# Softplus of the stick-breaking units in its symmetric form: the clip on VectorE goes, an absolute value on ScalarE comes

## The chip, the cores and the metric

One core of a Trainium2 chip runs the whole program. The metric is the device time of one execution in microseconds (us); less is better. The kernel before takes 1800.53 us, the median of three runs.

## What is computed

The program is a stack of transformer layers on 512 tokens of width 1024 in fp32. The change lies in the first layer, in its stick-breaking attention: 8 heads of width 64, blocks of 128 queries, each block against all keys up to its end.

```python
logits = einsum("bqhd,bkhd->bhqk", q_block, k[:, :k_end]) * scale
strict = (q_start + arange(128))[:, None] > arange(k_end)[None, :]
log_beta = log_sigmoid(logits)
log_keep = where(strict, log_sigmoid(-logits), 0.0)
log_tail = cumsum(log_keep, axis=3, reverse=True) - log_keep
weights = where(strict, exp(log_beta + log_tail), 0.0)
out = einsum("bhqk,bkhd->bqhd", weights, v[:, :k_end])
```

Since log_sigmoid(-x) = -softplus(x), a softplus of every logit is wanted. All else in the program (another attention before it, projections, three feed-forward blocks, two more layers' attention) is the same in both kernels.

## The kernel before

The whole program is written out by hand: each of the engines TensorE (PE), VectorE (DVE), ScalarE (ACT), GpSimd (POOL) and SyncE (SP) has one list of instructions in a fixed order, and semaphores join the lists. An engine that waits at one instruction does nothing that stands behind it.

The stick-breaking attention is worked off in 16 units, `SB_UNITS`. Unit u is a pair of heads p = u // 4 and a step r = u % 4 over the keys, the last block of keys first. Its logits are [128 keys, 2 heads, 128 (r + 1) queries], so the units of a pair hold 256, 512, 768 and 1024 elements a partition. They lie in PSUM at `sb_psum(u)`, in two banks of their own for each r. What the engines do for unit u:

- PE, `sb_qk(u)` (L1048, and L1051 for the mask, which adds a large negative number where a key isn't strictly before its query): the logits x. It waits until the weights of unit u - 4 have been read (`sb_weights`).
- DVE, L2521: `sb_clip(u)` = min(x, 40) into one of two buffers in `tmp` (`sb_clamped`).
- ACT, `softplus` (L1607, L1609): Exp and then Ln(1 + .) in place on that buffer (`sb_exped`, `sb_logged`).
- DVE, `sb_larger(u)` (L2484): max(x, that) into `sb_pl`, one of three buffers (`sb_plus`). This is softplus(x), since above 40 softplus(x) is x.
- PE, `sb_tail_sum(u)` (L1061 with a triangle, and L1070 with ones for the units of the pair so far): the suffix sums, added onto the logits in PSUM. Where r is 2 or more the ones meet a running sum that DVE makes in `sb_add` (L2499, L2500).
- ACT, `sb_weigh(u)` (L1772): Exp of that, from PSUM into `sb_w`.
- PE, `sb_values(p)` (L1079), once for each pair, one unit late: the weights against the values, into bank 6. ACT, `sb_save(p)` (L1778), copies it out, and PE's `sb_qk` of a unit with r = 3 waits for that copy.

The order on the engines: for u = 0 to 17 ACT does sb_weigh(u - 2), softplus(u), and sb_save at u = 5, 9 and 13 (then, at u = 8, 12 and 16, a square of the saved tile). DVE does sb_larger(u - 1), clip(u), sb_add(u - 1), but where u % 4 is 3 the clip(u) comes ahead of sb_larger(u - 1). PE does sb_tail_sum(u) and, after it, sb_qk(u + 3), except that sb_qk of r = 3 stands in the middle of the tail sum two units before. Other work lies among these: at u = 0 ACT squares a tile and splits a weight chunk (L1502), at u = 1 it takes a square root, for which it loads another table of functions and then the first again (L1796); at u = 12 ACT and DVE scale and split four tiles; and at u = 15 PE does part of the product with w_out (L868 to L870). Behind the last unit the root over the attention's output is needed before PE can go on.

Of the kernel before, what the change touches and what calls it, by code (L numbers as in the profile page):

```python
# [15 lines left out]
ALU = mybir.AluOpType  # L16
AXIS = mybir.AxisListType
ACT = mybir.ActivationFunctionType

P = 128  # L20
SEQ = 512
# [15 lines left out]
CLAMP = 40.0  # L37
# [30 lines left out]
ADD0 = {name: sum(n - 1 for _, n in NORMS[:i]) for i, (name, _) in enumerate(NORMS)}  # L68
# [33 lines left out]
def program(nc, a, out):  # L102
    ctx = ExitStack()
    with ctx:
        def at(name, shape, offset, dt=FP32):
            return nc.alloc_sbuf_tensor_at(name, shape, dt, offset=offset)

        def sem(name):
            return ctx.enter_context(nc.semaphore(name))
# [13 lines left out]
        sb_pl = at("sb_pl", [P, 3, 2, SEQ], o_act)  # L123
# [193 lines left out]
        def modv(section, t):  # L317
# [39 lines left out]
        sq_added = sem("sq_added")  # L357
# [12 lines left out]
        mem_diag, mem_tile, mem_done, mem_saved = (  # L370
            sem("mem_diag"), sem("mem_tile"), sem("mem_done"), sem("mem_saved"))
# [22 lines left out]
        out_hi, q_tile, q_saved = sem("out_hi"), sem("q_tile"), sem("q_saved")  # L394
        mem_q_saved = sem("mem_q_saved")

        sb_scores, sb_clamped, sb_exped, sb_logged, sb_plus = (
            sem("sb_scores"), sem("sb_clamped"), sem("sb_exped"), sem("sb_logged"), sem("sb_plus"))
        sb_tail, sb_weights, sb_out, sb_saved, sb_added = (
            sem("sb_tail"), sem("sb_weights"), sem("sb_out"), sem("sb_saved"), sem("sb_added"))  # L400

# [331 lines left out]
        SB_UNITS = 4 * 4  # L733

        def sb_unit(u):

            p, r = u // 4, u % 4
            return p, r, P * (3 - r)

        def sb_psum(u):  # L740

            b = (2, 4, 0, 6)[u % 4]
            return banks[:, b:b + 2, sb_unit(u)[2]:SEQ]

        SB_OUT = 6

        def sb_clip(u):

            return tmp[:, 2 * (u % 2):2 * (u % 2) + 2, sb_unit(u)[2]:SEQ]

# [744 lines left out]
        def _(act):  # L1495
# [8 lines left out]
            def split_at(c, n=2048):  # L1504
                split_w(c, c % 2, 16 * (c // 2 + 1), n)
# [11 lines left out]
            def square(name, t, src, ready):  # L1517
                n = NORM[name]
                act.wait_ge(*ready)
                if t == 0:  # L1520
                    if n:
                        act.wait_ge(sum_ready, n)
                    act.activation(sq_sum[:, :], src, ACT.Square).then_inc(sq_ready, 1)
                else:
                    if t >= 3:
                        act.wait_ge(sq_added, ADD0[name] + t - 2)
                    act.activation(squares_of(name, t), src, ACT.Square).then_inc(sq_ready, 1)

            def root(name):
                n, count = NORM[name], NORMS[NORM[name]][1]  # L1530
                act.wait_ge(sum_ready, n + 1)
                act.activation(rms[:, :], norm_bank(name), ACT.Sqrt, scale=-1.0 / (P * count), bias=eps)\
                    .then_inc(root_ready, 1)

            def high(name, t, dst, bias=None, buf=tmp):

                act.wait_ge(scaled, SPLIT0[name] + t + 1)
                act.activation(dst, buf[:, t % 4, :], ACT.Identity,
                               bias=bias if bias is not None else 0.0).then_inc(act_hi_done, 1)
# [61 lines left out]
                    if beside:  # L1601
                        beside(t)

            def softplus(t, clamped, exped, logged, n):

                act.wait_ge(clamped, n)
                act.activation(t, t, ACT.Exp).then_inc(exped, 1)  # L1607
                act.wait_ge(exped, n)
                act.activation(t, t, ACT.Ln, bias=1.0).then_inc(logged, 1)  # L1609

# [155 lines left out]
            def sb_weigh(u):  # L1766

                p, r, q0 = sb_unit(u)
                act.wait_ge(sb_tail, u + 1)
                if p >= 2 and r == 0:  # L1770
                    act.wait_ge(sb_out, p - 1)
                act.activation(sb_w[:, p % 2, :, P * r * (r + 1) // 2:P * (r + 1) * (r + 2) // 2],  # L1772
                               sb_psum(u), ACT.Exp).then_inc(sb_weights, 1)

            def sb_save(p):

                act.wait_ge(sb_out, p + 1)
                act.activation(o_raw[1][:, p, :], bank[SB_OUT], ACT.Copy).then_inc(sb_saved, 1)  # L1778

            def square_b(p):  # L1780
                square("ob", p, o_raw[1][:, p, :], (sb_saved, p + 1))

            for u in range(SB_UNITS + 2):
                if u >= 2:
                    sb_weigh(u - 2)
                if u < SB_UNITS:
                    softplus(sb_clip(u), sb_clamped, sb_exped, sb_logged, u + 1)
                if u == 0:
                    square("oa", 3, o_raw[0][:, 3, :], (out_saved, 4))
                    split_at(C0["w_out"] + 1)  # L1790
                if u in (5, 9, 13):
                    sb_save(u // 4 - 1)
                if u == 1:
                    act.preload_act_table(ACT.Sqrt)
                    root("oa")
                    act.preload_act_table_set("natural_log_exp_and_others")  # L1796
                if u in (8, 12, 16):
                    square_b(u // 4 - 2)
                if u == 12:
                    for t in range(4):  # L1800
                        high("w_out", t, o_hi_0[0][:, t, :], buf=rel[0])
# [140 lines left out]
        def _(dve):  # L1942
# [306 lines left out]
            for t in range(NT):  # L2249
                if t:  # L2250
                    dve.wait_ge(x_squared, t)
                dve.tensor_tensor_reduce(out=x_junk, in0=x_tok[:, t, :], in1=x_tok[:, t, :], scale=1.0,
                                         scalar=0.0, op0=ALU.mult, op1=ALU.add,
# [33 lines left out]
            def mem_save(c, m):  # L2287
                dst = (kmT_0, vm_0)[c % 2][c // 2]
                dve.wait_ge(mem_done if m else mem_tile, c + 1)
                return dve.tensor_copy(dst[:, m, :], bank[mem_bank(c, m)][:, 0:NMEM])  # L2290
# [12 lines left out]
            for n in range(4):  # L2303
# [6 lines left out]
                                     op0=ALU.add, op1=ALU.add).then_inc(scaled, 8)  # L2310
# [165 lines left out]
            def sb_larger(u):  # L2476

                p, r, q0 = sb_unit(u)
                dve.wait_ge(sb_logged, u + 1)
                if u == 0:  # L2480
                    dve.wait_ge(chunk_done, C0["w_out"])
                if u >= 3:
                    dve.wait_ge(sb_tail, u - 1 if r == 3 else u - 2)
                dve.tensor_tensor(sb_pl[:, u % 3, :, q0:SEQ], sb_psum(u), sb_clip(u), ALU.max)\  # L2484
                    .then_inc(sb_plus, 1)

            def sb_add(u):

# [21 lines left out]
                                  ALU.subtract).then_inc(act_ready, 1)  # L2510

            for u in range(SB_UNITS + 1):
                if u and u % 4 != 3:
                    sb_larger(u - 1)
                if u < SB_UNITS:
                    if u == 0:
                        dve.wait_ge(sq_added, ADD0["oa"] + 2)
                    if u == 2:
                        mem_save(1, 1).then_inc(mem_saved, 1)
                    dve.wait_ge(sb_scores, u + 1)  # L2520
                    dve.tensor_scalar(sb_clip(u), sb_psum(u), CLAMP, None, ALU.min).then_inc(sb_clamped, 1)  # L2521
                if u % 4 == 3:
                    sb_larger(u - 1)
                if u and (u - 1) % 4 in (1, 2):
                    sb_add(u - 1)
                if u == 1:
                    mem_save(1, 0).then_inc(mem_saved, 1)
                    add_squares("oa", 3)
                    split_w(C0["w_out"] + 1, 1)
                if u in (13, 16):  # L2530
                    add_squares("ob", 1 + u // 16)
                for n in {4: (0,), 5: (1,), 8: (2,), 9: (3,)}.get(u, ()):
                    c = P * n
                    dve.wait_ge(root_ready, NORM["oa"] + 1)
                    part = dve.reciprocal(rms[:, c:c + P], rms[:, c:c + P])
                    if n == 3:
                        part.then_inc(rms_ready, 1)
                if u == 12:
                    dve.wait_ge(rms_ready, NORM["oa"] + 1)
                    for t in range(4):  # L2540
                        scale_a(t)
                    low_a(0)
                    low_a(1)
                if u == 13:
                    low_a(2)
                    low_a(3)
# [38 lines left out]
            for t in range(KT):  # L2585
                dve.scalar_tensor_tensor(out=x[:, t, :], in0=x[:, t, :], scalar=gain("final_g", t),
                                         in1=rms[:, :], op0=ALU.mult, op1=ALU.mult).then_inc(x_ready, 1)
            split_w(C0["a_q"], 0)
            for t in range(NT):
                dve.wait_ge(av_saved, NT + t + 1)  # L2590
                if t:
                    dve.wait_ge(v_ss, t)
                dve.tensor_tensor_reduce(out=vsq_junk[:, :], in0=vtok_a[:, t, :], in1=vtok_a[:, t, :], scale=1.0,
                                         scalar=0.0, op0=ALU.mult, op1=ALU.add,
# [39 lines left out]
            for ct in range(6):  # L2634
# [4 lines left out]
                for lo, hi, g in gm_parts(ct):  # L2639
                    dve.scalar_tensor_tensor(  # L2640
                        out=tmp[lo:hi, ct % 2, :].rearrange("p (n t) -> p n t", t=P),
                        in0=gm_bank(ct)[lo:hi, :].rearrange("p (n t) -> p n t", t=P),
                        scalar=vec[lo:hi, VEC0["a_v_norm_2"] + ct:VEC0["a_v_norm_2"] + ct + 1],
                        in1=bs[lo:hi, g, :].rearrange("p (o t) -> p o t", o=1)
# [161 lines left out]
```

## Time and profile before

| | |
|---|---|
| median of 3 runs | 1800.53 us |
| the three runs | 1802.06, 1800.53, 1800.51 us |
| the profiled execution: its time | 1800.57 us |
| its span, first to last instruction | 1798.9 us |
| TensorE's granted clock, mean over the span | 0.999 of full speed |
| span of the stick-breaking stage | about 214 us to 287 us from the start |

The span is what the trace covers; 1.67 us lie around it. Times in the trace are microseconds from the start of the span. PEld is TensorE's loading of weights, which overlaps its products. "Idle before" is the time in which an engine stood still just ahead of an instruction, and the name behind it is what ended that.

### The profile page before, as it was taken

The numbers are of one execution on the slowest core, as the hardware profiler recorded it, in microseconds if no ns is written. First come the engines' busy times: TensorE is split into PE (matmuls) and PEld (weight loads), VectorE is DVE, ScalarE is ACT, GpSimd is POOL, SyncE is SP. The second block draws the span as 40 slices with busy tenths as digits, with TensorE's granted clock in tenths as the row PEclk, the third lists the DMA queues.
The fourth block names the chain that finished last, engine by engine and source line by source line (L and its number), as shares of the span: only waits on it lengthen the run. The fifth ranks groups of instructions, "written<-read, shape, count | busy, mean of one in ns | idle before, by whom it ended". The sixth has DMA issues, their size and how long they took to land.

```text
span 1798.9 us, 22457 instructions
## 1 busy us (share of the span) xinstructions
PE 1768.7 (98%) x8312; PEld 1428.7 (79%) x8312; DVE 1096.3 (61%) x1598; ACT 733.2 (41%) x1030; POOL 40.6 (2%) x78
## 2 busy tenths in 40 slices
PE   7999999999999999999999999999999999999998
PEld 6887547888888888878888888889766888888887
DVE  6878775655556335775677674245577567677423
ACT  7313663333444223444344443233365434444322
POOL 4110000000000000000000000000000000000000
PEclk9999999999999999999999999999999999999999
DMA  9794203232222323312322222323401232222231
GB/s 345 266 340 139 80 21 111 75 106 94 93 93 87 111 82 98 112 48 94 117 93 93 93 93 84 109 83 106 170 24 48 74 114 93 93 93 93 94 105 70
DMA packets 149081, 195.29 MB, mean 109 GB/s; under 512 B 3646, under 2 KB 133000, under 8 KB 146332
## 3 DMA queue, kind: packets, MB, share of 16 engines
q1 hardware_dynamic: 140696, 154.23, 26.4%
q0 software_dynamic: 7600, 39.13, 5.9%
q10 hardware_dynamic: 724, 1.10, 0.2%
q8 instruction: 41, 0.67, 0.2%
q14 instruction: 20, 0.16, 0.0%
HBM read 189.15 MB, written 5.29 MB: 108 GB/s over the span
## 4 chain that ended last, share of the span: by engine, by line
PE 92%; DVE 4%; DMA 2%; ACT 1%; issue 1%; POOL 0%; DVEq 0%; ACTq 0%
PE bank L805 20%; PE bank L807 20%; PE bank L806 20%; PE bank L868 3%; PE bank L870 3%; PE bank L869 3%; PE bank L1475 2%; PE bank L1474 2%; PE bank L1476 2%; PE bank L952 2%; PE bank L1004 1%; PE bank L848 1%; PE bank L973 1%; PE bank L849 1%; PE bank L850 1%; PE bank L1061 1%
## 5 line engine op out<-in xcount | busy, mean ns | idle before, releaser
L1947 DVE TENSOR_TENSOR w_lo<-w_stage,w_hi 128x2048 fp32r<-128x2048 f32 (+3 forms) x136 | 299.0, 2198 | 436.3 <-ACT w_hi L1502 436.0
L805 PE MATMUL bank<-act_hi,w_hi 128*128 128x512 f32 x1216 | 475.2, 391 | 1.5 <-DVE act_lo L2322 0.6
L807 PE MATMUL bank<-act_hi,w_lo 128*128 128x512 f32 x1216 | 473.3, 389 | 0.0
L806 PE MATMUL bank<-act_lo,w_hi 128*128 128x512 f32 x1216 | 473.1, 389 | 0.0
L1502 ACT ACTIVATE w_hi<-w_stage 128x2048 fp32r<-128x2048 f32 (+3 forms) x138 | 253.6, 1837 | 466.0 <-PE bank L807 335.6
L805 PEld LDWEIGHTS bank<-act_hi,w_hi 128*128 128x128 f32 x1216 | 228.2, 188 | 50.7 <-DVE act_lo L2011 2.1
L806 PEld LDWEIGHTS bank<-act_lo,w_hi 128*128 128x128 f32 x1216 | 228.3, 188 | 47.7 <-issue 0.5
L807 PEld LDWEIGHTS bank<-act_hi,w_lo 128*128 128x128 f32 x1216 | 228.2, 188 | 47.7
L805 PE MATMUL bank<-mid_hi,w_hi 128*128 128x512 f32 x352 | 136.9, 389 | 0.0
L806 PE MATMUL bank<-mid_lo,w_hi 128*128 128x512 f32 x352 | 136.9, 389 | 0.0
L807 PE MATMUL bank<-mid_hi,w_lo 128*128 128x512 f32 x352 | 136.9, 389 | 0.0
L1649 ACT ACTIVATE mid_hi<-tmp 128x512 f32 x66 | 40.7, 633 | 97.1 <-DVE tmp L2157 97.1
L806 PEld LDWEIGHTS bank<-mid_lo,w_hi 128*128 128x128 f32 x352 | 66.1, 188 | 13.8
L805 PEld LDWEIGHTS bank<-mid_hi,w_hi 128*128 128x128 f32 x352 | 66.1, 188 | 13.8
L807 PEld LDWEIGHTS bank<-mid_hi,w_lo 128*128 128x128 f32 x352 | 66.1, 188 | 13.6
L1474 PE MATMUL bank<-w_hi,mid_hi 128*128 128x512 f32 x176 | 68.8, 391 | 0.0
L1476 PE MATMUL bank<-w_lo,mid_hi 128*128 128x512 f32 x176 | 68.5, 389 | 0.0
L1475 PE MATMUL bank<-w_hi,mid_lo 128*128 128x512 f32 x176 | 68.5, 389 | 0.0
L1639 ACT ACTIVATE tmp<-tmp,vec 128x512 f32<-128x512 f32 x44 | 33.5, 809 | 70.0 <-DVE tmp L1969 70.0
L1639 ACT ACTIVATE mid_val<-tmp,vec 128x512 f32 x44 | 33.5, 808 | 69.8 <-DVE tmp L1969 69.8
L1969 DVE SCALAR_TENSOR_TENSOR tmp<-bank,rms 128x512 f32<-128x512 f32 x88 | 56.4, 682 | 0.0
L2161 DVE TENSOR_TENSOR mid_lo<-tmp,mid_hi 128x512 f32 x66 | 42.7, 689 | 9.4 <-ACT mid_hi L1649 9.4
(412 smaller groups left out, 2622.8 us busy)
## 6 DMA issues: line engine op xcount, KB each, us to landing
ada_stage<-in_w_ada POOLq DMA_DIRECT2D x24, 1024.0 KB, 7.4
w_stage<-in_w_up SPq DMA_DIRECT2D x22, 1024.0 KB, 5.0
w_stage<-in_a_ffn_in SPq DMA_DIRECT2D x22, 1024.0 KB, 5.0
w_stage<-in_b_ffn_in SPq DMA_DIRECT2D x22, 1024.0 KB, 5.1
w_stage<-in_w_in SPq DMA_DIRECT2D x10, 1024.0 KB, 7.6
w_stage<-in_b_ffn_out SPq DMA_DIRECT2D x10, 1024.0 KB, 5.1
w_stage<-in_w_down SPq DMA_DIRECT2D x8, 1024.0 KB, 5.1
w_stage<-in_a_ffn_out SPq DMA_DIRECT2D x8, 1024.0 KB, 5.1
```

Of the source, the lines that this page charges most:

```text
L805: pe.matmul(dst, wh, mh, start=start and k == 0, stop=False)
L806: pe.matmul(dst, wh, ml, start=False, stop=False)
L807: last = pe.matmul(dst, wl, mh, start=False, stop=stop and k == nk - 1)
L868: pe.matmul(dst, wh, mh, start=start and k == ks[0], stop=False)
L869: pe.matmul(dst, wh, ml, start=False, stop=False)
L1474: pe.matmul(dst, mh, hi[:, k, :], start=j == 0 and k == 0, stop=False)
L1475: pe.matmul(dst, ml, hi[:, k, :], start=False, stop=False)
L1476: last = pe.matmul(dst, mh, lo[:, k, :], start=False, stop=j == 5 and k == nk - 1)
L1502: act.activation(w_hi[slot][:, 0:n], raw[:, 0:n], ACT.Copy).then_inc(w_hi_done, 1)
L1639: act.activation(conv_tile(f, i, s, m), conv_src(f, s, m)[:, :], ACT.Identity, scale=w2, bias=b).then_inc(tap_started, 1)
L1947: dve.tensor_tensor(w_lo[slot][:, 0:n], raw[:, 0:n], w_hi[slot][:, 0:n].bitcast(FP32), ALU.subtract).then_inc(w_ready, 1)
L1969: return dve.scalar_tensor_tensor(out=dst, in0=src[:, :], scalar=scale, in1=norm[:, :], op0=ALU.mult, op1=ALU.mult)
```

## The change

The softplus is taken as max(x, 0) + log(1 + exp(-|x|)). ScalarE takes |x| from PSUM (`sb_size`), then Exp with a scale of -1, then Ln as before; VectorE's clip goes, and its `sb_larger` becomes one instruction that takes the maximum with 0 and adds. Since VectorE no longer has a step for unit u, `sb_larger(u - 1)` isn't behind one either for any u. The copies of the output (`sb_save`) stay where they are, on ScalarE.

```diff
-        def sb_clip(u):
+        def sb_abs(u):
...
-            def softplus(t, clamped, exped, logged, n):
+            def softplus(t, clamped, exped, logged, n, sign=1.0):
                 act.wait_ge(clamped, n)
-                act.activation(t, t, ACT.Exp).then_inc(exped, 1)
+                act.activation(t, t, ACT.Exp, scale=sign).then_inc(exped, 1)
...
+            def sb_size(u):
+
+                act.wait_ge(sb_scores, u + 1)
+                if u == 0:
+                    act.wait_ge(sq_added, ADD0["oa"] + 2)
+                if u >= 2:
+                    act.wait_ge(sb_plus, u - 1)
+                act.activation(sb_abs(u), sb_psum(u), ACT.Abs).then_inc(sb_sized, 1)
...
                 if u >= 2:
                     sb_weigh(u - 2)
                 if u < SB_UNITS:
-                    softplus(sb_clip(u), sb_clamped, sb_exped, sb_logged, u + 1)
+                    sb_size(u)
+                    softplus(sb_abs(u), sb_sized, sb_exped, sb_logged, u + 1, -1.0)
...
-                dve.tensor_tensor(sb_pl[:, u % 3, :, q0:SEQ], sb_psum(u), sb_clip(u), ALU.max)\
-                    .then_inc(sb_plus, 1)
+                dve.scalar_tensor_tensor(out=sb_pl[:, u % 3, :, q0:SEQ], in0=sb_psum(u), scalar=0.0,
+                                         in1=sb_abs(u), op0=ALU.max, op1=ALU.add).then_inc(sb_plus, 1)
...
             for u in range(SB_UNITS + 1):
-                if u and u % 4 != 3:
+                if u:
                     sb_larger(u - 1)
-                if u < SB_UNITS:
-                    if u == 0:
-                        dve.wait_ge(sq_added, ADD0["oa"] + 2)
-                    if u == 2:
-                        mem_save(1, 1).then_inc(mem_saved, 1)
-                    dve.wait_ge(sb_scores, u + 1)
-                    dve.tensor_scalar(sb_clip(u), sb_psum(u), CLAMP, None, ALU.min).then_inc(sb_clamped, 1)
-                if u % 4 == 3:
-                    sb_larger(u - 1)
+                if u == 2:
+                    mem_save(1, 1).then_inc(mem_saved, 1)
                 if u and (u - 1) % 4 in (1, 2):
                     sb_add(u - 1)
```

## Rows read from the trace of the kernel before

**Rows 1.** The page: busy time by engine, the last chain by engine, one group of instructions

```profile
PE 1768.7 (98%) x8312; PEld 1428.7 (79%) x8312; DVE 1096.3 (61%) x1598; ACT 733.2 (41%) x1030; POOL 40.6 (2%) x78
...
PE 92%; DVE 4%; DMA 2%; ACT 1%; issue 1%; POOL 0%; DVEq 0%; ACTq 0%
...
L1969 DVE SCALAR_TENSOR_TENSOR tmp<-bank,rms 128x512 f32<-128x512 f32 x88 | 56.4, 682 | 0.0
```

**Rows 2.** Busy time of each engine in two stretches, with granted clock

```profile
217.00:230.00 13.00, 12.67 (x62) 8.74 (x61) 9.90 (x15) 12.00 (x15) 0.55 (x1) 1.00 0.30 102
...
243.00:256.00 13.00, 13.00 (x66) 6.81 (x65) 7.68 (x13) 7.84 (x13) 0.00 (x0) 1.00 0.01 1
```

**Rows 3.** Timeline of ScalarE, first units: start, us, instruction, idle before

```profile
215.48 1.28 ACT L1764 ACT_TABLE_LOAD   x1
...
221.16 1.28 ACT L1794 ACT_TABLE_LOAD   x1
...
224.45 0.38 ACT L1772 ACTIVATE sb_w<-bank 128x256 f32<-128x256 f32 x1
...
226.13 0.84 ACT L1609 ACTIVATE tmp<-tmp 128x768 f32<-128x768 f32 x1
```

**Rows 4.** Pieces of the chain that ended last, in order of time: start, us, what

```profile
228.02 1.56 PE bank L1061 x4
...
234.38 0.84 PE bank L1048 x4
...
242.77 1.56 PE bank L1061 x4
...
246.04 1.77 PE bank L1061 x4
247.82 1.29 PE bank L1070 x4
249.11 0.85 PE bank L1048 x4
...
250.67 2.30 PE bank L1079 x16
...
257.50 1.56 PE bank L1061 x4
...
272.22 1.56 PE bank L1061 x4
...
276.02 1.72 PE bank L1061 x4
```

**Rows 5.** Timeline of VectorE, units 6 and 7

```profile
240.63 1.23 DVE L2521 TENSOR_SCALAR tmp<-bank 128x1024 f32<-128x1024 f32 x1 [1.88 <-PE bank L1051]
241.77 0.95 DVE L2484 TENSOR_TENSOR sb_pl<-bank,tmp 128x768 f32<-128x768 f32 x1
...
244.06 1.23 DVE L2484 TENSOR_TENSOR sb_pl<-bank,tmp 128x1024 f32<-128x1024 f32 x1 [0.42 <-ACT tmp L1609]
```

**Rows 6.** Timeline of ScalarE, units 5 to 7

```profile
238.30 0.60 ACT L1778 ACTIVATE ob_raw<-bank 128x512 f32<-128x512 f32 x1 [1.68 <-PE bank L1079]
...
239.93 0.84 ACT L1609 ACTIVATE tmp<-tmp 128x768 f32<-128x768 f32 x1
241.13 0.60 ACT L1772 ACTIVATE sb_w<-bank 128x512 f32<-128x512 f32 x1 [0.35 <-PE bank L1070]
...
242.97 1.06 ACT L1609 ACTIVATE tmp<-tmp 128x1024 f32<-128x1024 f32 x1
```

**Rows 7.** Groups by line and shape, 200 to 300 us: busy us, mean ns, idle before

```profile
L1772 ACT ACTIVATE sb_w<-bank 128x1024 f32<-128x1024 f32 x4 | 4.1, 1018 | 7.0 <-PE bank L1070 7.0
...
L1772 ACT ACTIVATE sb_w<-bank 128x768 f32<-128x768 f32 x4 | 3.2, 812 | 4.3 <-PE bank L1070 4.3
...
L2504 DVE SCALAR_TENSOR_TENSOR rel<-oa_raw,vec,rms 128x512 f32<-128x512 f32 x4 | 2.7, 746 | 0.0
```

**Rows 8.** The instructions of line 2521, the clip: ns min/median/max

```profile
L2521 DVE TENSOR_SCALAR tmp<-bank x16: 414/814/1225, 213.9 to 270.1; 128x256 f32<-128x256 f32 x4, 128x512 f32<-128x512 f32 x4, 128x768 f32<-128x768 f32 x4, 128x1024 f32<-128x1024 f32 x4
```

More of the change, by code:

```diff
@@ L395, in program @@
         mem_q_saved = sem("mem_q_saved")
-        sb_scores, sb_clamped, sb_exped, sb_logged, sb_plus = (
-            sem("sb_scores"), sem("sb_clamped"), sem("sb_exped"), sem("sb_logged"), sem("sb_plus"))
+        sb_scores, sb_sized, sb_exped, sb_logged, sb_plus = (
+            sem("sb_scores"), sem("sb_sized"), sem("sb_exped"), sem("sb_logged"), sem("sb_plus"))
         sb_tail, sb_weights, sb_out, sb_saved, sb_added = (
```

## The prediction

> **What bounds the kernel now.** I read the page first. TensorE is busy for 1768.7 of 1798.9 us, and 92% of the chain that ended last is its work [rows 1]: the kernel is one long line of products, and a change elsewhere counts only where TensorE comes to stand and wait. Next, the busy times in windows of the stick-breaking stage. In the first units (217 to 230 us) ScalarE is busy for 12.00 of 13 us, in a later pair of heads (243 to 256) for 7.84 [rows 2]; VectorE has room in both. So ScalarE's room for one more step is not the same everywhere. Last, the chain and the two timelines. Three times TensorE stands still ahead of the tail sum of a unit with r = 2, at 242.77, 257.50 and 272.22, with 14.73 and 14.72 us between them [rows 4]: that distance is the period of a pair. What it waits for is sb_larger(6), which starts at 241.77 though its Ln ended at 239.93 + 0.84 = 240.77; the clip of unit 7 lay ahead of it from 240.63 [rows 5, 6]. Elsewhere in the pair TensorE doesn't wait.
>
> **What goes.** 16 clips on VectorE, four of each size, median 814 ns [rows 8]: 13.0 us of VectorE's time. Of this only the clips of units 3, 7, 11 and 15 lie on the path, and with them gone sb_larger(6) could start 1.0 us sooner. That is the gain: at most 1 us a pair.
>
> **What comes.** 16 times Abs on ScalarE, from PSUM into SBUF. No row shows an Abs. The nearest rows are sb_weigh, which is an activation of the same shapes over the same route: 0.38 us for 256 elements [rows 3], 0.60 for 512 [rows 6], 0.81 and 1.02 for 768 and 1024 [rows 7]; and sb_save, a Copy, is 0.60 for 512 as well [rows 6]. I take these, since Exp and Copy cost the same: 4 × 2.81 = 11.2 us more on ScalarE. Each Abs stands between sb_weigh(u - 2) and Exp(u). Where two neighbours in a queue don't depend on each other, the next starts about 0.1 before the end of the one before (on VectorE 241.77 against 240.63 + 1.23 [rows 5]); Abs now starts so behind sb_weigh, as Exp did, and Exp starts 0.03 after the end of Abs, as Ln after Exp. So every unit's way is longer by its Abs and 0.03. Bounds: an Abs that took no time, below; above, the pass from SBUF (Ln, 1.06 for 1024 [rows 6]), 0.04 more each.
>
> Exp with a scale of -1 and Ln keep their durations. sb_larger becomes a SCALAR_TENSOR_TENSOR. With an immediate scalar and a source in PSUM it takes 682 ns for 512 elements [rows 1], which is what the clip and the maximum of such a row cost (0.95 for 768, 1.23 for 1024 [rows 5]): nothing more. With a scalar from a tile it takes 746 [rows 7], the upper bound, 0.06 more.
>
> The new waits of Abs(u), for sb_scores and for sb_larger(u - 2), end early: the logits of unit 7 are there before the old clip starts at 240.63 [rows 5], and Abs(7) comes some 3 us later. That of sq_added at u = 0 ends before the table load at 215.48 is over. Behind the Abs stand Exp, Ln and the next sb_weigh; VectorE's sb_larger and then TensorE's tail sum wait for them.
>
> **The sum, first units.** Here ScalarE is the bound. Abs(0) adds 0.38 + 0.03 and Abs(1) 0.60 + 0.03, so sb_weigh(0) goes from 224.45 [rows 3] to 225.49 and ends at 225.87. Abs(2) 225.77 to 226.58, Exp(2) to 227.45, Ln(2) to 228.32 (it was 226.13 + 0.84 = 226.97 [rows 3]), sb_larger(2) 228.35 to 229.30. The tail sum of unit 2 starts at 229.34 instead of 228.02 [rows 4]: **+1.32**. Then sb_weigh(1) to 228.82, Abs(3) to 229.74, Exp(3) 230.83, Ln(3) 231.92, sb_larger(3) 233.18. TensorE, done with unit 2 and sb_qk(5) at 232.61, has to wait for this. A tail sum of 768 elements takes 1.56 after a wait [rows 4], where three quarters of the 1.72 that 1024 take would be 1.29; so a wait costs 0.27 of filling, and after one 1024 take some 1.99. Tail sum 3 is done at 233.22 + 1.99 + 1.29 = 236.50; it was 234.38, where sb_qk(6) starts [rows 4]: **+2.12**. Covers are gone from here on.
>
> **The sum, a pair.** Everything up to the values of pair 0 is late by 2.12, so sb_save(0) starts at 238.30 + 2.12 = 240.42 [rows 6] and ends at 241.02. sb_weigh(4) to 241.30, Abs(6) to 242.01, Exp 242.88, Ln 243.75, sb_larger(6) 244.73, tail sum 6 at 244.77, for 242.77 before: +2.00. The clip that no longer lies ahead of sb_larger(6) pays for the Abs, and 0.12 is over. But then: sb_weigh(5) to 244.25, Abs(7) to 245.17, Exp 246.26, Ln(7) 247.35 (it was 242.97 + 1.06 = 244.03 [rows 6]), sb_larger(7) 248.61. Tail sum 7 starts at 248.65, not 246.04 [rows 4], and TensorE is free 0.6 before that: the wait moves from r = 2 alone to r = 2 and r = 3. Its end is 251.93 for 249.11: **+2.82**, 0.70 more than a pair ago. The period can be read in one loop, from Ln(6) to Ln(10): sb_weigh(5) 0.50, Abs(7) 0.92, Exp and Ln(7) 2.18, sb_larger(7) 1.26, tail sum 7 0.04 + 1.99 + 1.29, sb_qk(10) 1.07, tail sum 8 0.50, values 2.30, sb_save 0.65, sb_weigh(8) 0.28, Abs(10) 0.71, Exp and Ln(10) 1.74, together 15.4 against 14.7. So pair 2 ends at +3.5.
>
> **The sum, last pair.** At u = 12 the four scaled tiles hold ScalarE as before, and TensorE still finds its inputs there. Tail sum 14 comes at values(2) + 4.4 = 275.6 for 272.22 (+3.4; without sb_qk behind it TensorE had waited longer here before), and tail sum 15, where part of the product with w_out gives cover, at about 279.5 for 276.02: **+3.5 to +3.7**. Behind it values, sb_save, the root and the scaling follow one another with no slack, and after that TensorE is the bound, so nothing is given back. I take +3.6.
>
> The profiled execution of before took 1800.57 (1798.9 + 1.67), 0.04 over the median of its runs. 1800.53 + 3.6 gives 1804.1 us. About 10 Abs lie on this path, so each 0.1 us by which one differs from my rows moves the result by 1.0 to 1.2. With both upper bounds (0.04 and 0.06 for each) it is +4.4. With an Abs of no time it is -1.7.
>
> The Trainium skill speaks against the change: the page "ScalarE: Activation LUTs", section "Rules for kernel authors", wants such cheap operations on VectorE, which it calls up to three times faster in bf16. The rows here are fp32 from PSUM and don't show that (clip 1.23 us for 1024 elements, ScalarE 1.02); what makes the change dear by my sum is the place in ScalarE's queue, not the rate.
>
> **The rivals.** (a) *The wait goes and nothing takes its place.* If Abs(7), Exp and Ln of unit 7 were hidden behind TensorE's work, the wait of some 1 us at three units would go. For it speaks that ScalarE stands idle for 5 of 13 us in a pair [rows 2]; against it that this idle time lies behind, not ahead of, the chain from sb_weigh(5) to Ln(7). It decides at an Abs 0.4 us shorter than my rows (no change in total), and at the bound of no time it gives 1798.9.
> (b) *Part of the delay is taken back*: Abs runs somewhat shorter, or the waits overlap. At 0.1 to 0.2 us less for each, 1801.9 to 1802.8.
> (c) *Abs brings table loads.* A load is 1.28 us [rows 3]; two a unit, to it and back, are 32 × 1.28 = 41 us, nearly all on the path: 1845. Against it: Copy runs between Exps with no load around it [rows 6].
> The same page, section "Table sets: the hidden batching unit", lists abs as a filler in every set, so that no load would come. No row of before shows an Abs.
> (d) *More than the sum*: dearer gaps between dependent activations, 0.1 instead of 0.03 on each Abs, and both upper bounds above: 1805 to 1806. That the longer waits make the granted clock fall is not likely, for it is 1.00 in both windows [rows 2].
>
> **Numbers.** My forecast, +3.0 to +4.4, has 0.72; (a) 0.04, (b) 0.13, (c) 0.02, (d) 0.09. The range of 8 in 10 takes in (b) in part and most of (d): 1801.8 to 1806.0. A measurement of this kernel can tell about 0.2%, 3.6 us, from no change, and my sum lies just there: I give half of the forecast's 0.72 to each side. Slower by over 0.2%: 0.37 + 0.11 = 0.48. Within: 0.35 + 0.13 + 0.02 = 0.50. Faster: 0.02.
>
> **What would show it.** In the profile after: 16 Abs with 0.38, 0.60, 0.81, 1.02 us and no new table load; sb_weigh(0) near 225.5; tail sum 3 ending near 236.5; the distance of the tail sums of units 6, 10 and 14 near 15.4; TensorE waiting for sb_larger at r = 2 and r = 3. I am wrong if Abs has another duration, if the wait at r = 3 is absent, or if the delay at 287 us is not that of the end.

## The result and the profile after

The changed kernel takes 1805.47 us in the median of 12 runs (1804.21 to 1808.47), the kernel before 1801.00 over 12 runs (1800.51 to 1802.06): a ratio of 1.0024, 95% interval 1.0015 to 1.0032. That is 4.5 us more, or 0.24%. It is just over the 0.2% named in the prediction, but the interval reaches to both sides of that mark. 1804.1 was forecast, within 1801.8 to 1806.0. The measured time lies in that range, but above the forecast's own band of +3.0 to +4.4, where the prediction had its rival (d).

The first lines of the page after: busy time by engine, and the shares of the chain that ended last.

```profile
PE 1771.0 (98%) x8312; PEld 1430.0 (79%) x8312; DVE 1084.7 (60%) x1582; ACT 743.2 (41%) x1046; POOL 40.6 (2%) x78
...
PE 91%; DVE 4%; ACT 2%; issue 1%; DMA 1%; SPq 0%; DVEq 0%; ACTq 0%
```

Against [rows 1]: VectorE does 16 instructions and 11.6 us less, ScalarE 16 and 10.0 us more, and ScalarE has 2% of the chain where it had 1%. TensorE's work is the same 8312 products, yet its busy time is 2.3 us more. The prediction's sum has only the filling after a wait for this; 1.5 us of it are one tail sum at a lower clock, which comes up below.

The groups by shape, 200 to 300 us, have the durations of Abs (busy us, mean ns, idle before), of which the kernel before has none:

```profile
L1787 ACT ACTIVATE tmp<-bank 128x1024 f32<-128x1024 f32 x4 | 4.1, 1015 | 0.0
...
L1787 ACT ACTIVATE tmp<-bank 128x768 f32<-128x768 f32 x4 | 3.3, 815 | 0.0
...
L1787 ACT ACTIVATE tmp<-bank 128x512 f32<-128x512 f32 x4 | 2.4, 588 | 0.0
```

They are those of sb_weigh for the same shapes [rows 7], 1018 and 812 ns. The timeline of ScalarE in the first units (start, us, instruction), to be held against [rows 3]:

```profile
215.42 1.28 ACT L1764 ACT_TABLE_LOAD   x1
216.72 0.38 ACT L1787 ACTIVATE tmp<-bank 128x256 f32<-128x256 f32 x1
217.13 0.42 ACT L1607 ACTIVATE tmp<-tmp 128x256 f32<-128x256 f32 x1
...
225.44 0.38 ACT L1772 ACTIVATE sb_w<-bank 128x256 f32<-128x256 f32 x1
225.72 0.81 ACT L1787 ACTIVATE tmp<-bank 128x768 f32<-128x768 f32 x1
226.55 0.84 ACT L1607 ACTIVATE tmp<-tmp 128x768 f32<-128x768 f32 x1
227.43 0.84 ACT L1609 ACTIVATE tmp<-tmp 128x768 f32<-128x768 f32 x1
```

Exp starts 0.02 to 0.03 us after the end of Abs, no table load stands between them, and sb_weigh(0) is at 225.44 where it was at 224.45 (225.49 was forecast). What TensorE makes of this is in its timeline; in brackets is the idle time before. These are all its waits for sb_larger:

```profile
229.32 2.23 PE L1061 MATMUL bank<-sb_pl,neg_upper 128*128 128x384 f32 x4 [1.60 <-DVE sb_pl L2494]
...
245.57 1.56 PE L1061 MATMUL bank<-sb_pl,neg_upper 128*128 128x384 f32 x4 [0.94 <-DVE sb_pl L2494]
...
249.42 1.98 PE L1061 MATMUL bank<-sb_pl,neg_upper 128*128 128x512 f32 x4 [0.57 <-DVE sb_pl L2494]
...
260.98 1.56 PE L1061 MATMUL bank<-sb_pl,neg_upper 128*128 128x384 f32 x4 [0.94 <-DVE sb_pl L2494]
...
264.82 1.98 PE L1061 MATMUL bank<-sb_pl,neg_upper 128*128 128x512 f32 x4 [0.57 <-DVE sb_pl L2494]
...
276.44 1.56 PE L1061 MATMUL bank<-sb_pl,neg_upper 128*128 128x384 f32 x4 [1.58 <-DVE sb_pl L2494]
```

Two things are to be read here. The waits at r = 2 (768 elements, "128x384" a head) have stayed, and those at r = 3 ("128x512") have come to them; the distance of the waits at r = 2 is 15.41 and 15.46 us against 14.73 and 14.72 [rows 4]. And the first row, tail sum 2, takes 2.23 us where the same four products take 1.56 everywhere else. The windows say why (start and end, length, busy us of PE, PEld, DVE, ACT, POOL, then the granted clock, 1.00 being full speed):

```profile
217.00:229.30 12.30, 10.64 (x55) 7.30 (x53) 6.26 (x10) 12.05 (x17) 0.55 (x1) 1.00 0.32 108
229.30:233.30 4.00, 3.98 (x10) 2.27 (x10) 2.31 (x4) 2.49 (x4) 0.00 (x0) 0.59 0.00 1
233.30:238.30 5.00, 5.00 (x21) 2.36 (x22) 1.95 (x3) 2.88 (x6) 0.00 (x0) 0.98 0.00 0
```

Behind the 1.60 us of waiting TensorE had the lower of its two clock levels, 1.2 GHz, for most of 4 us. Narrower windows show when:

```profile
227.70:229.30 1.60, 0.01 (x1) 0.00 (x0) 0.96 (x2) 1.60 (x3) 0.00 (x0) 1.00 0.06 18
229.30:230.00 0.70, 0.68 (x2) 0.49 (x3) 0.70 (x2) 0.67 (x2) 0.00 (x0) 1.00 0.02 6
230.25:233.25 3.00, 3.00 (x9) 1.55 (x7) 1.37 (x2) 1.56 (x2) 0.00 (x0) 0.50 0.00 0
233.50:238.30 4.80, 4.80 (x21) 2.16 (x20) 1.75 (x3) 2.68 (x6) 0.00 (x0) 1.00 0.00 0
```

The clock is full during the wait and for the first 0.7 us of products behind it, and falls only then, with TensorE busy. In the kernel before the clock is 1.00 in this stage. So the profiled execution, 1805.20 us, holds one such fall; how often the runs do is a question for the experiments.

### The profile page after: what moved, and what is told of

The parts are those of the page before. It is cut to its first block, busy times and chain, and to the rows that moved or that the text cites. A ratio compares the mean times of both kernels' runs of the same rounds, so it can differ in the third digit from the quotient of the medians.

```text
span 1803.5 us, 22471 instructions
## 1 busy us (share of the span) xinstructions
PE 1771.0 (98%) x8312; PEld 1430.0 (79%) x8312; DVE 1084.7 (60%) x1582; ACT 743.2 (41%) x1046; POOL 40.6 (2%) x78
## 4 chain that ended last, share of the span: by engine, by line
PE 91%; DVE 4%; ACT 2%; issue 1%; DMA 1%; SPq 0%; DVEq 0%; ACTq 0%
PE bank L805 20%; PE bank L807 20%; PE bank L806 20%; PE bank L868 3%; PE bank L870 3%; PE bank L869 3%; PE bank L1476 2%; PE bank L1475 2%; PE bank L1474 2%; PE bank L952 2%; PE bank L1004 1%; PE bank L973 1%; PE bank L848 1%; PE bank L849 1%; PE bank L850 1%
```

## The experiments

A measure of its own was wanted, since half a microsecond is less than the scatter of times. In each trace I take the stretch from the start of ScalarE's copy ahead of the first units (L1567, oa_raw) to the start of its root behind the last (L1532, rms). Everything that the change touches lies in it, and what happens in the 214 us ahead doesn't. That matters: from trace to trace the stretch starts anywhere between 214.49 and 216.57 us, while what lies behind it is 1512.2 to 1512.6 us in all of them. The stretch is 286.57 - 214.86 = 71.71 us before and 291.08 - 214.81 = 76.27 after: +4.56. In the table "reckoned" is what was forecast for the kernel, "stretch" the difference of the stretch to 71.71, one trace each, and "median" the difference to the median of the kernel before in the same session (11 runs of each kernel, 5 of the one with every Abs twice).

```
kernel                               reckoned  stretch   median   ratio, 95% interval
the change                             +3.6     +4.56     +4.5    1.0024 (1.0015-1.0032)
Abs on VectorE in the clip's place      0       -0.03     +0.7    1.0000 (0.9991-1.0009)
clip kept, sb_larger always first      +3.2     +3.06     +3.0    1.0017 (1.0008-1.0026)
change in pair 0 alone                 +2.1     +2.09     +3.6    1.0019 (1.0010-1.0028)
change in pairs 1 to 3 alone           +1.5     +1.61     +1.5    1.0008 (0.9999-1.0017)
Abs ahead of sb_weigh                  +2.3     +2.53     +2.1    1.0013 (1.0004-1.0022)
copies on VectorE                      +2.2     +2.60     +2.0    1.0014 (1.0004-1.0023)
both                                   +0.1     +0.39     -0.3    1.0001 (0.9992-1.0010)
change, TensorE's first wait filled  +3.6-4.0   +3.72     +3.4    1.0019 (1.0010-1.0029)
every Abs twice                       +10.8    +12.66    +12.1    1.0078 (1.0064-1.0091)
pick: clip for pair 0 and r = 2        -1.5     -1.34     -1.8    0.9992 (0.9983-1.0001)
pick: clip for pair 0, copies moved    -1.5     -1.47     -2.1    0.9991 (0.9982-1.0000)
pair 0 alone, first wait filled      +2.0-2.3   +2.08     +1.6    1.0012 (1.0003-1.0021)
```

The cuts of code below are against the kernel before in the first two experiments and against the changed kernel in the others; "..." stands for lines left out.

**Formula or place.** The symmetric formula with its absolute value on VectorE, in the place and order of the clip. |x| is taken there by clearing the sign bit.

```diff
-                    dve.tensor_scalar(sb_clip(u), sb_psum(u), CLAMP, None, ALU.min).then_inc(sb_clamped, 1)
+                    dve.tensor_scalar(sb_abs(u).bitcast(mybir.dt.int32), sb_psum(u).bitcast(mybir.dt.int32),
+                                      0x7fffffff, None, ALU.bitwise_and).then_inc(sb_clamped, 1)
```

> The symmetric softplus with its absolute value on VectorE, in the place and order of the old clip; Exp with scale -1 and the new sb_larger stay. If the loss comes from where Abs stands in ScalarE's queue, this costs nothing: within 0.3 us of the kernel before, tail sums of units 2, 6, 10 and 14 at the times of before (228.0, 242.8, 257.5, 272.2), and no fall of the clock. If the formula itself costs (Exp with a scale, an add more in sb_larger), some 1 us or more stays. If the order of sb_larger had been the cause, this is 0 as well.

The stretch is 71.68 us, that of before to 0.03. The timeline of TensorE has the waits of before, in their places [rows 4]:

```profile
228.04 1.56 PE L1070 MATMUL bank<-sb_pl,neg_upper 128*128 128x384 f32 x4 [0.26 <-DVE sb_pl L2502]
...
242.79 1.56 PE L1070 MATMUL bank<-sb_pl,neg_upper 128*128 128x384 f32 x4 [1.04 <-DVE sb_pl L2502]
```

The median is 0.7 higher, with an interval of 0.9991 to 1.0009; nothing in the trace answers to it. Exp with a scale of -1 and the combined sb_larger cost nothing: the whole loss is that of the move to ScalarE, or of the order.

**The order.** The old formula and clip, and only sb_larger(u - 1) always ahead of the clip of u.

```diff
-                if u and u % 4 != 3:
+                if u:
                     sb_larger(u - 1)
...
-                if u % 4 == 3:
-                    sb_larger(u - 1)
```

> The old formula with the old clip, only sb_larger(u - 1) is always ahead of clip(u), as in the changed kernel. The text of the change makes this look like the part that helps. By the same reckoning from durations as the prediction's: sb_larger(6) is 1 us sooner, but clip(7) now lies behind it, so Exp(7), Ln(7) and sb_larger(7) come later and TensorE waits at r = 3: +0.6 after tail sum 6, +2.1 after tail sum 7, +3.2 us in all. The rival, that the clip ahead of sb_larger was what held TensorE, gives -1 us for each of three units, -3 us.

+3.06, not -3. In this trace the stretch starts 0.83 us later than in that of before, and so do all times in it. VectorE's timeline (first fence) and ScalarE's (second) around unit 7 show the exchange:

```profile
243.11 0.96 DVE L2506 TENSOR_TENSOR sb_pl<-bank,tmp 128x768 f32<-128x768 f32 x1 [2.06 <-ACT tmp L1618]
243.99 1.22 DVE L2548 TENSOR_SCALAR tmp<-bank 128x1024 f32<-128x1024 f32 x1
```

```profile
245.24 1.06 ACT L1616 ACTIVATE tmp<-tmp 128x1024 f32<-128x1024 f32 x1 [1.21 <-DVE tmp L2548]
```

sb_larger(6) now comes at once, but clip(7) behind it lets Exp(7) wait for 1.21 us, where it had been 0.16 before. In pairs 1 and 2 TensorE now waits for 1.30 us at r = 3 instead of 1.04 at r = 2; pair 0 has a new wait of 1.29 at r = 3, and the last pair 0.70 and 0.76 in place of 1.68. So the clip in front of sb_larger was the right order as long as there was a clip. The change can put sb_larger first only because it leaves no clip behind it.

**The first units and the others.** The new form for units 0 to 3 alone, and for 4 to 15 alone; the others keep clip, maximum and order.

```diff
+        def sb_new(u):
+            return u < 4          # the other kernel: u >= 4
...
+                    if sb_new(u):
+                        sb_size(u)
...
+                if not sb_new(u):
+                    dve.tensor_tensor(sb_pl[:, u % 3, :, q0:SEQ], sb_psum(u), sb_abs(u), ALU.max)\
+                        .then_inc(sb_plus, 1)
+                    return
```

> The change for units 0 to 3 alone; units 4 to 15 have the clip as before. My sum: +2.1 us, all of it by the end of tail sum 3, and nothing after it. If the granted clock falls after the wait ahead of tail sum 2, as in the profile of the changed kernel, +2.9. If the loss were spread evenly over the units (a cost for each Abs), a quarter of it by time of work: +1.1.

> The change for units 4 to 15 alone. My sum: +1.5 us (0.7 a pair for two pairs, little in the last), the clock at full speed throughout, distance of tail sums 6, 10 and 14 of 15.4 against 14.7 us. By an even cost of each Abs: +3.4. Together with the run for pair 0 it should add to the whole change.

The stretches are +2.09 and +1.61, together +3.70. So four of 16 units have more than half of the loss, as ScalarE's 12.00 of 13 us in [rows 2] had let one expect. In the profile of pair 0 alone the clock stays up, and the sum of the prediction can be read in TensorE's timeline without it:

```profile
229.29 1.56 PE L1070 MATMUL bank<-sb_pl,neg_upper 128*128 128x384 f32 x4 [1.60 <-DVE sb_pl L2509]
...
233.14 1.98 PE L1070 MATMUL bank<-sb_pl,neg_upper 128*128 128x512 f32 x4 [0.57 <-DVE sb_pl L2509]
```

Forecast were 229.34 and 233.22, and 1.99 for the second. But the median, +3.6, is 1.5 above this trace, and six of its eleven runs are over 1.5 us above the fastest: that calls for a second cause, which the profiled execution didn't meet. The mean granted clock of each run hints at the clock: it is 0.998 in five of those six and 0.999 in the five others.

**The queue.** From unit 2 on Abs(u) ahead of sb_weigh(u - 2); the copies of pairs 0 to 2 on VectorE; both together.

```diff
+                if 2 <= u < SB_UNITS:
+                    sb_size(u)
                 if u >= 2:
                     sb_weigh(u - 2)
```

```diff
-                if u in (5, 9, 13):
-                    sb_save(u // 4 - 1)
...
+                if u in (6, 10, 14):
+                    dve.wait_ge(sb_out, u // 4)
+                    dve.tensor_copy(o_raw[1][:, u // 4 - 1, :], bank[SB_OUT]).then_inc(sb_saved, 1)
```

> The changed kernel, but from unit 2 on Abs(u) stands ahead of sb_weigh(u - 2) instead of behind it. If the place in ScalarE's queue is the cause, an Abs that falls into ScalarE's wait for a tail sum is hidden: for r = 0 and 1 there is such a wait, for r = 2 and 3 there is hardly one, since there ScalarE is what sets the pace. Reckoned as in the prediction: +0.4 by tail sum 3 less than the change, distance of tail sums 6, 10 and 14 of 15.15 instead of 15.4 us, +2.3 us to before in all where the change has +3.5. If the mere work of ScalarE is the bound, moving it changes nothing (+3.5).

> The changed kernel, but the copies of the output (sb_save of pairs 0 to 2) are on VectorE. ScalarE then no longer stands waiting for the values (2.3 us on TensorE) and for its copy ahead of sb_weigh(4), so the loop of 15.4 us is cut between tail sum 8 and Abs(10): the wait at r = 2 goes, that at r = 3 grows to 1.3 us, distance 15.0 us, +2.2 us in all. By the rival that VectorE's copy is itself late for sb_qk of r = 3: no better than the change.

> Both: Abs ahead of sb_weigh, and the copies on VectorE. Reckoned: 1.4 to 1.5 us lost in the first units (these are not touched by it), then a distance of 14.4 us, less than the 14.7 of before, and +0.1 us in all: equal to the kernel before. If the two gains were the same time counted twice, +2.

The same 16 Abs with the same durations cost +2.5, +2.6 and +0.4. With both moves the waits at r = 2 beyond pair 0 are gone, and the distance of tail sums 7, 11 and 15 is 14.38 and 14.43 us, under the 14.7 of before:

```profile
248.26 1.98 PE L1061 MATMUL bank<-sb_pl,neg_upper 128*128 128x512 f32 x4 [0.69 <-DVE sb_pl L2495]
...
262.64 1.98 PE L1061 MATMUL bank<-sb_pl,neg_upper 128*128 128x512 f32 x4 [0.69 <-DVE sb_pl L2495]
...
277.07 1.98 PE L1061 MATMUL bank<-sb_pl,neg_upper 128*128 128x512 f32 x4 [0.87 <-DVE sb_pl L2495]
```

ScalarE's timeline in the same kernel has Abs(7) straight behind a wait, ahead of sb_weigh(5), and Exp(7) right behind sb_weigh(5):

```profile
243.41 1.02 ACT L1787 ACTIVATE tmp<-bank 128x1024 f32<-128x1024 f32 x1 [1.42 <-PE bank L1051]
244.33 0.59 ACT L1772 ACTIVATE sb_w<-bank 128x512 f32<-128x512 f32 x1
244.80 1.06 ACT L1607 ACTIVATE tmp<-tmp 128x1024 f32<-128x1024 f32 x1
```

The forecasts for the three kernels were 0.2 to 0.4 us too low. The order of ScalarE's work, and not its amount, is what the change costs in pairs 1 to 3.

**How much each Abs counts.** Every Abs is done a second time, on its own result.

```diff
-                act.activation(sb_abs(u), sb_psum(u), ACT.Abs).then_inc(sb_sized, 1)
+                act.activation(sb_abs(u), sb_psum(u), ACT.Abs).then_inc(sb_half, 1)
+                act.wait_ge(sb_half, u + 1)
+                act.activation(sb_abs(u), sb_abs(u), ACT.Abs).then_inc(sb_sized, 1)
```

> The changed kernel with every Abs done twice, the second time in place in SBUF (the absolute value of an absolute value, so nothing of the result changes). 11.2 us more on ScalarE. With my account all but the last of it lies on the path: each unit's way is longer by its Abs again, TensorE waits at r = 1, 2 and 3, +7 us more than the change, about +10.8 us to before. If ScalarE's idle time took it up, +1 to +3 more than the change. If all of it and more counted, +11 more.

The stretch grows by 8.1 us over the change's for some 12 us more on ScalarE, where 7 had been reckoned: some two thirds of this further work lie on the path. The second pass reads SBUF and starts 0.03 after the first, which I had left out of the reckoning. A fall of the clock, as after, is in this trace too (the first four products of tail sum 2 take 2.06 us, after a wait of 2.57).

**The clock.** Two products more on TensorE in the first wait, into columns that nobody reads; first in the changed kernel ahead of tail sum 2, then in that of pair 0 alone, ahead of the logits of unit 4.

```diff
+                if u == 2:
+                    for n in range(2):
+                        pe.matmul(bank[2][:, 0:384], neg_upper[:, :], qkv[:, 16, 0:384], start=False,
+                                  stop=True, skip_group_check=True)
                 sb_tail_sum(u)
```

> The changed kernel with two products more on TensorE in the wait ahead of tail sum 2 (into columns of a bank that nobody reads; 1.3 us of work in a wait of 1.6), which change no time by themselves. If a fall of the granted clock after that wait is what lifts the median of the changed kernel 0.9 us over my sum, the runs lie closer together and the median is 0.5 to 0.9 us under the change's 1805.5; the profile has the clock at full speed. If the fall has no part in it, the time is the change's, or up to 0.3 above.

> The kernel with the change in pair 0 alone, and two products more on TensorE (1.3 us) ahead of the logits of unit 4, so that TensorE waits some 0.3 us ahead of tail sum 2 and not 1.6. Nothing that the chain needs comes later by them. Without them it was 1804.5 us in the median, but 1802.7 in the profiled execution, where the clock stayed up. If a fall of the clock is what lies between the two, the median comes down to 1802.8 to 1803.5, +2.0 to +2.3 to before. If the scatter has another cause, it stays near 1804.5.

With the fill the wait ahead of tail sum 2 is 0.26 us, and the clock is 1.00 in the whole stage:

```profile
230.15 1.56 PE L1061 MATMUL bank<-sb_pl,neg_upper 128*128 128x384 f32 x4 [0.26 <-DVE sb_pl L2498]
```

The stretch is +3.72, which is 0.84 less than the change's, and the prediction's sum was +3.6. The fill costs nothing itself: pair 0 alone has +2.08 with it and +2.09 without. Set against this execution of the change, the fall cost 0.84 us. But two traces without the fill, that of pair 0 alone and that with the copies on VectorE, wait for the same 1.60 us at the same place and keep their clock. The window that was at 0.59 in the change reads in the first of them:

```profile
229.30:233.30 4.00, 3.43 (x15) 2.01 (x16) 2.31 (x4) 3.20 (x4) 0.00 (x0) 1.00 0.00 0
```

1.00, and 15 products in the time of 10. So the fall came in one of three traces with this wait: the wait doesn't force it. The medians agree in direction: 1805.47 goes to 1804.82 with the fill (ratios 1.0024 and 1.0019), and pair 0 alone from +3.6 to +1.6 (1.0019 and 1.0012). But the intervals overlap, and the kernel before was 1800.93 in the one session and 1801.66 in the other. As a whole the profiled execution with the fill, 1805.45 us, wasn't faster than the change's, 1805.20, for its stretch starts at 215.65 us and not at 214.81. That the fall costs 0.84 us in the trace that has it is shown. That it makes the scatter of the runs, and that the fill takes it away, isn't shown. The runs without a profile don't say where the clock fell, and there is a second place: in the first 50 us it is 0.97 in three traces, those with clip and sb_larger first, with both moves and with the fill, and 1.00 in the others. Pair 0 alone with the fill still has two runs of eleven at 1805.2 and 1805.5 with mean clocks of 0.997 and 0.998.

**What they point to.** The clip stays where ScalarE has no room. First: pair 0 and r = 2 keep the clip, the rest has Abs ahead of sb_weigh. Second: pair 0 alone keeps it, Abs ahead of sb_weigh, copies on VectorE.

```diff
         def sb_new(u):
+            return u >= 4 and u % 4 != 2          # the second: u >= 4
```

> What the experiments point to: the clip on VectorE stays for pair 0, where ScalarE is the bound, and for r = 2; the new form with Abs ahead of sb_weigh for r = 0, 1 and 3 of pairs 1 to 3. Copies stay on ScalarE. sb_larger(6) isn't behind a clip any more, and Abs(7) lies in time that ScalarE has. Reckoned: -1.5 us to before. The rival: the wait only moves to r = 3, 0.

> The clip stays for pair 0 alone; pairs 1 to 3 have the new form with Abs ahead of sb_weigh, and the copies are on VectorE. It is the run with both moves, less what that lost in the first units: -1.5 us to before. If that loss doesn't go with pair 0, 0.

The stretches are -1.34 and -1.47 us, the medians 1799.38 and 1799.12 against 1801.20: a tenth of a per cent, and both intervals just reach 1. TensorE's waits in the first of the two, ahead of tail sums 2, 7, 11 and 14:

```profile
228.23 1.56 PE L1070 MATMUL bank<-sb_pl,neg_upper 128*128 128x384 f32 x4 [0.25 <-DVE sb_pl L2508]
...
245.73 1.98 PE L1070 MATMUL bank<-sb_pl,neg_upper 128*128 128x512 f32 x4 [0.43 <-DVE sb_pl L2511]
...
260.14 1.98 PE L1070 MATMUL bank<-sb_pl,neg_upper 128*128 128x512 f32 x4 [0.43 <-DVE sb_pl L2511]
...
270.91 1.56 PE L1070 MATMUL bank<-sb_pl,neg_upper 128*128 128x384 f32 x4 [0.73 <-DVE sb_pl L2508]
```

1.8 us of waiting are left of the 4.0 of before (0.26, 1.04, 1.04 and 1.68 in the trace with Abs on VectorE, whose stretch is that of before). Of these 2.2 us 1.34 reach the stretch; where the rest goes wasn't followed.

## Why the prediction was right, point by point

- *Abs costs what sb_weigh costs.* 815 and 1015 ns for 768 and 1024 elements; right, and so were the 0.03 to Exp. The Trainium skill, page "ScalarE: Activation LUTs", section "Table sets: the hidden batching unit", names abs as a filler of every set; the trace agrees, with no load between the Abs and Exp rows above and 21 table loads in the program before and after. Rival (c) is out.
- *The new sb_larger and Exp cost nothing.* Shown by Abs on VectorE: -0.03 us. That kernel is also the answer to the Trainium skill, page "ScalarE: Activation LUTs", section "Rules for kernel authors", which wants relu, max, min, add and mul on VectorE. The clip, a min, is one of these; an absolute value isn't in the list. VectorE is the better place in this kernel, but not by speed: there the step takes 1226 ns for 1024 elements (the row below, Abs on VectorE), on ScalarE 1015.

```profile
L2541 DVE TENSOR_SCALAR tmp<-bank 128x1024 int32<-128x1024 int32 x4 | 4.9, 1226 | 5.0 <-PE bank L1060 4.9
```

- *First units, +1.32 and +2.12.* With the clock up, tail sum 2 starts at 229.29 and tail sum 3 at 233.14 (pair 0 alone), each within 0.1 of the forecast, and the stretch is +2.09.
- *A pair, 15.4 us.* 15.41 and 15.46; the waits are 0.94 at r = 2 and 0.57 at r = 3, and the latter was forecast at 0.6. Pairs 1 to 3 alone give +1.61, for a sum of +1.5.
- *Nothing is given back after the stage.* The stretch is +4.56 and the span of the trace 4.6 us longer (1803.5 against 1798.9).
- *The last pair.* Tail sum 14 starts at 276.44. Less the 0.84 of the fall that is 275.60, and 275.6 was forecast.
- *+3.6 in all.* +3.72 in the trace with the fill, in which the clock stays up. Of the change's +4.56, 0.84 is the fall.
- *The clock.* This is the step that failed. I wrote under (d) that a fall of the granted clock "is not likely", on the evidence of two windows at 1.00. It was thin evidence: TensorE stands still for 0.33 us in the one and not at all in the other, and the waits of 1.04 and 1.68 us of that trace lie outside both. The clock fell in the profile, after 1.60. Of the 1.4 us between 1804.1 and 1805.47, 0.5 is that twelve runs of before lie at 1801.0 and not at the 1800.53 of three; the other 0.9 has the size of the fall in that one trace, which doesn't show that it is the fall in the twelve. Its price was small, since while TensorE ran slowly its wait for sb_larger(3), 0.57 us, went under: tail sum 2 took 1.5 more (3.86 us to the next logits, against 2.36 in pair 0 alone), and the stage 0.84.
- *The forecast and the range.* The mechanism came true term by term, but the number lies in the range only because that took in most of (d): 1805.47 is within (d)'s 1805 to 1806, which had a chance of 0.09, and over the +3.0 to +4.4 that had 0.72. What (d) was made of, dearer gaps and dearer instructions, isn't what came: the gaps are 0.02 to 0.03, and sb_larger takes 958 and 1225 ns for 768 and 1024 elements. In this the range was lucky. The two halves of the 0.72 were put down as 0.37 and 0.35 where half is 0.36, which changes nothing.
- *Rival (a)*, that the idle time would take Abs up, is out for the change as written. It holds in pairs 1 to 3 once Abs stands ahead of sb_weigh and the copies are elsewhere (14.38 us a pair): what had been said against it, that the idle time lies at another place in the queue, is then gone.

## What to carry to other kernels

An operation moved to the engine with more idle time can lose, though it is faster there, if that engine's idle time lies behind the instruction it is put in front of. Look at the queue unit by unit: what it pushes back, where that engine waits, and whether the new step's inputs are there early enough to stand in that wait. And a new wait on TensorE can cost more than its own length: the one of 1.60 us here cost 0.84 us more in the one trace of three in which the clock fell behind it.

## What was not expected of the hardware

TensorE's clock fell to 1.2 GHz after a wait of 1.60 us, in a stage in which it had been busy for 10.64 of 12.30 us. It fell between 230.00 and 230.25 us, 0.7 to 0.9 us after the wait was over. With every Abs twice it fell too, between 232.00 and 232.25, 0.7 to 1.0 us behind a wait of 2.57. In two other traces with the wait of 1.60 and almost the same work ahead of it (10.62 of 12.30 us in pair 0 alone, 10.37 of 12.04 with the copies on VectorE) it didn't fall. The kernel before waits for 1.68 us ahead of tail sum 14 and kept its clock there in its trace, 1.00 from 268 to 277 us with TensorE busy for 7.32 of 9.00. What decides between these stays open.
